# Rotary tables made during the second block's layer-0 closing feed-forward; latent preparation in another order

## What is computed

```python
def second_block(x, mem, positions, ...):
    cos, sin = rope_tables(positions)
    for layer in range(DEPTH_2):
        if layer == N_A_LAYERS:
            shared = shared_mla_kv(x, ..., cos, sin)
        x = x + FFN_HALF * swiglu(rms_norm(x, norm_g[layer, 0]), ...)
        h = rms_norm(x, norm_g[layer, 1])
        if layer < N_A_LAYERS:
            y_mix, q_mem = short_conv_mixer(h, ...)
        else:
            q_nope, q_rope, q_mem = mla_queries(h, ..., cos, sin)
            y_mix = causal_mla_attention(q_nope, q_rope, k_nope, k_rope, v)
        y_mem = memory_attention(q_mem, mem, ...)
        x = x + jnp.concatenate([y_mix, y_mem], axis=-1) @ w_out[layer]
        x = x + FFN_HALF * swiglu(rms_norm(x, norm_g[layer, 2]), ...)

def rope_tables(positions):
    inv_freq = ROPE_THETA ** (-jnp.arange(0, QK_ROPE_DIM, 2) / QK_ROPE_DIM)
    ang = positions[..., None] * inv_freq
    return jnp.cos(ang), jnp.sin(ang)
```

## Time and profile before

| | us |
|---|---|
| median of 3 runs | 3041.64 (3040.64 to 3044.88) |
| the profiled execution, device time | 3040.44 |
| its span, first to last instruction | 3038.2 |
| PE busy | 2986.5 |
| DVE busy | 1828.8 |
| ACT busy | 943.8 |
| POOL busy | 231.7 |
| mean granted clock of PE | 0.996 |

### The profile page before, as it was taken

One profiled execution on the slowest core, in us unless ns is written; L12 is line 12 of the kernel. 1 busy time (PEld: TensorE's weight loads), 2 busy tenths in 40 slices (PEclk: granted clock), 3 DMA queues, 4 the chain that ended last, 5 costly groups with the idle time before them and its releaser, 6 DMA issues.

```text
span 3038.2 us, 36195 instructions
## 1 busy us (share of the span) xinstructions
PE 2986.5 (98%) x13373; PEld 2418.5 (80%) x13373; DVE 1828.8 (60%) x2405; ACT 943.8 (31%) x1279; POOL 231.7 (8%) x107
## 2 busy tenths in 40 slices
PE   8999999999999999999999999999999998999999
PEld 7787788788888887888787888887888875688887
DVE  8896565567766546554587655446554467665532
ACT  4643632333222222222223222222222235322222
POOL 0043240000000000000032000002000022000000
PEclk9999999999999999999999999999999999999999
DMA  4222223233322222223332222332223321122232
GB/s 146 97 93 81 68 97 117 67 103 105 97 97 97 97 97 88 96 95 105 113 107 70 90 97 97 104 104 95 92 97 104 104 87 63 35 90 97 97 104 97
DMA packets 79305, 287.55 MB, mean 95 GB/s; under 512 B 8992, under 2 KB 9248, under 8 KB 78816
## 3 DMA queue, kind: packets, MB, share of 16 engines
q1 hardware_dynamic: 77904, 280.06, 27.5%
q0 software_dynamic: 1296, 6.03, 0.6%
HBM read 283.96 MB, written 2.10 MB: 94 GB/s over the span
## 4 chain that ended last, share of the span: by engine, by line
PE 83%; issue 10%; DVE 5%; POOL 2%; ACT 1%; DMA 0%; POOLq 0%; ACTq 0%; DVEq 0%
PE ps L663 26%; PE ps L665 26%; PE ps L664 26%; POOL w_lo L622 2%; PE ps L1052 1%; PE ps L1297 0%; DVE w_lo L1846 0%; PE ps L1260 0%; DMA mem_x<-in_mem 0%; ACT w_hi L1344 0%; PE ps L833 0%; PE ps L727 0%; PE ps L1041 0%; DVE small L1997 0%; PE ps L947 0%
## 5 line engine op out<-in xcount | busy, mean ns | idle before, releaser
L1344 ACT ACTIVATE w_hi<-raw 128x1024 fp32r<-128x1024 f32 x524 | 554.4, 1058 | 1385.7 <-PE ps L665 1383.5
L663 PE MATMUL ps<-h_hi,w_hi 128*128 128x512 f32 (+1 forms) x2379 | 935.1, 393 | 8.7 <-DVE w_lo L1846 3.3
L665 PE MATMUL ps<-h_hi,w_lo 128*128 128x512 f32 (+1 forms) x2379 | 924.3, 389 | 0.0
L664 PE MATMUL ps<-h_lo,w_hi 128*128 128x512 f32 (+1 forms) x2379 | 924.3, 389 | 0.0
L1846 DVE TENSOR_TENSOR w_lo<-raw,w_hi 128x1024 fp32r<-128x1024 f32 x434 | 530.7, 1223 | 473.9 <-ACT w_hi L1344 473.1
L663 PEld LDWEIGHTS ps<-h_hi,w_hi 128*128 128x128 f32 x2379 | 448.4, 188 | 115.7 <-issue 13.5
L665 PEld LDWEIGHTS ps<-h_hi,w_lo 128*128 128x128 f32 x2379 | 447.8, 188 | 93.0
L664 PEld LDWEIGHTS ps<-h_lo,w_hi 128*128 128x128 f32 x2379 | 448.2, 188 | 92.0 <-issue 2.6
L663 PE MATMUL ps<-mid_hi,w_hi 128*128 128x512 f32 x1208 | 470.8, 390 | 2.2 <-DVE mid_lo L1924 2.1
L664 PE MATMUL ps<-mid_lo,w_hi 128*128 128x512 f32 x1208 | 470.0, 389 | 0.0
L665 PE MATMUL ps<-mid_hi,w_lo 128*128 128x512 f32 x1208 | 470.0, 389 | 0.0
(11 more groups left out here) (409 smaller groups left out, 2471.7 us busy)
## 6 DMA issues: line engine op xcount, KB each, us to landing
raw<-in_wstream SPq DMA_DIRECT2D x525, 512.0 KB, 3.3
x<-in_x SPq DMA_DIRECT2D x4, 512.0 KB, 7.1
x_in<-in_x POOLq DMA_DIRECT2D x8, 256.0 KB, 3.2
mem_x<-in_mem POOLq DMA_DIRECT2D x2, 1024.0 KB, 5.1
out<-x SPq DMA_DIRECT2D x8, 256.0 KB, 4.5
tmp<-in_ret_decay POOLq DMA_DIRECT2D x1, 1024.0 KB, 5.0
rope_r<-in_rope_r POOLq DMA_DIRECT2D x1, 512.0 KB, 3.7
mats<-in_mats SPq DMA_DIRECT2D x1, 256.0 KB, 8.4
```

What stands on the lines that cost most here:

```text
L663: nc.tensor.matmul(dst, hi_w, hi_x, start=first, stop=False)
L664: nc.tensor.matmul(dst, hi_w, lo_x, start=False, stop=False)
L665: return nc.tensor.matmul(dst, lo_w, hi_x, start=False, stop=last)
L1344: nc.scalar.activation(w_hi[:, n % HL], raw[:, r], ACT.Copy).then_inc(hi_ready, 1)
```

## The change

1. POOL loads the positions before the run `conv0`, into `krope` (unused until `ckv`), and waits for them. 2. DVE makes the tables during `s0b_in` through `behind`: conversion, product and first table after pair c = 0, second table after pair c = 1. Work tiles are `ckv`; the result `rope2` lies in the padded rows of the convolution, `cpad`. 3. ACT takes the Sin between `s0b_in` and `s0b_out`. 4. The sums of `cq` come one panel and a half earlier, after the fourth panel of `mla_in`. 5. In `uq` the first two memory panels come first, the last two panels `uq` change places, and the rounds are placed anew; the norms of the last three query tiles come after the first two scores.

```diff
-MEM1_PANEL, MEM1_TILE = (2, 3, 7, 8), (10, 11, 17, 18)
-UQ_PANEL, UQ_TILE = (0, 1, 4, 5, 6), (2, 3, 6, 7, 12, 13, 14, 15, 16)
-V_TILE = (0, 1, 4, 5, 8, 9)
+MEM1_PANEL, MEM1_TILE = (0, 1, 7, 8), (2, 3, 17, 18)
+UQ_PANEL, UQ_TILE = (2, 3, 4, 6, 5), (4, 5, 8, 9, 12, 13, 15, 16, 14)
+V_TILE = (0, 1, 6, 7, 10, 11)
...
-                    rope2 = sb(a, "rope2", [P, 2, S])
...
+        rope2, angle, turns = cpad[:, :, 4:], ckv[:, 0], ckv[:, 1]
...
             pool.dma_start(mem_x[:], A["mem"]).then_inc(side_loaded, 16)
             pool.wait_ge(side_loaded, 48)
+            pool.dma_start(krope[:, 0].bitcast(I32), A["positions"].to_broadcast([P, S])).then_inc(side_loaded, 16)
+            pool.wait_ge(side_loaded, 64)
             split_run("conv0")
...
-            pool.wait_ge(side_loaded, 64)
-            pool.dma_start(rope2[:, 0].bitcast(I32), A["positions"].to_broadcast([P, S])).then_inc(side_loaded, 16)
             pool.wait_ge(side_loaded, 80)
             split_run("mla")
...
                 if j == 1:
                     spread_norms("ckv", "krope")
+                if j == 3:
+                    sums("cq")
...
                 if g == 0:
-                    sums("cq")
-                if g == 1:
                     spread_norms("cq")
             round_sums(1)
...
             v_turned_tiles(0)
-            uq_gemm(0)
+            mem1_gemm(0)
+            mem1_gemm(1)
             round_spread(1)
             round_sums(2)
+            uq_gemm(0)
             v_turned_tiles(2)
+            round_spread(2)
+            round_sums(3)
             uq_gemm(1)
-            round_spread(2)
             v_turned_tiles(4)
-            mem1_gemm(0)
-            mem1_gemm(1)
+            round_spread(3)
+            turn(krope[:, 0])
             uq_gemm(2)
-            round_sums(3)
+            uq_gemm(4)
+            round_sums(4)
             uq_gemm(3)
...
-            ffn("s0b")
+            silus("s0b_in", root)
+            act.wait_ge(sin_in, 2)
+            nc.scalar.activation(rope2, rope2, ACT.Sin).then_inc(sin_done, 1)
+            gemm("s0b_out", to_stage("s0b_out"), parts=3)
...
-            ffn("s0b", gain2(1, 0))
...
+            def rotary_tables(c):
+                if c == 0:
+                    dve.wait_ge(side_loaded, 64)
+                    done(v.tensor_copy(angle, krope[:, 0].bitcast(I32)))
+                    done(v.tensor_scalar(angle, angle, vcol("inv_freq", 0), None, ALU.mult))
+                    rotary_table(0, 0.25)
+                if c == 1:
+                    rotary_table(1, 0.0)
+
+            ffn("s0b", gain2(1, 0), behind=rotary_tables)
```

More of the change, by code:

```diff
@@ L1750, in _ @@
                     drain(st.n + g, st.t + 4 * g + m, (q_nope if m % 2 else k_nope)[:, hd])
[L1751 to L1754, removed]
-                    act.wait_ge(sin_in, 1)
-                    nc.scalar.activation(rope2[:, 0:2], rope2[:, 0:2], ACT.Sin).then_inc(sin_done, 1)
             st = ST["uq"]
@@ L1796, in _ @@
             round_squares(3, qm[:, 0], qm[:, 1], mem_k1_whole)
+            round_root(2)
+            aux[0] += 3
+            uq_drain(0)
+            v_copies(2)
+            round_root(3)
+            aux[0] += 4
+            uq_drain(1)
+            v_copies(4)
+            drained_up_to(UQ_TILE[3])
             uq_drain(2)
-            round_root(3)
-            aux[0] += 3
             drained_up_to(UQ_TILE[4])
             round_squares(4, *(q_rope[:, j] for j in range(3)))
-            uq_drain(3)
+            uq_drain(4)
+            drained_up_to(UQ_TILE[5])
+            round_squares(5, *(q_nope[:, hd] for hd in range(3)))
             round_root(4)
             aux[0] += 3
-            drained_up_to(UQ_TILE[5])
-            round_squares(5, *(q_nope[:, hd] for hd in range(3)))
-            uq_drain(4)
+            uq_drain(3)
+            drained_up_to(UQ_TILE[7])
+            round_squares(6, *(q_nope[:, hd] for hd in range(3, 6)))
             round_root(5)
             aux[0] += 4
-            drained_up_to(UQ_TILE[8])
-            round_squares(6, *(q_nope[:, hd] for hd in range(3, 6)))
             mem1_drain(2)
@@ L2570, in _, with rotary_table @@
             x_gemm("wo0", residual(1.0, "wo0", gain2(0, 2)), 3)
-            ffn("s0b", gain2(1, 0))
+            magic = 1.5 * 2.0 ** 23
+            c1 = 6.28125
+            c2 = float(np.float32(np.round((2 * np.pi - c1) * 2.0 ** 20) / 2.0 ** 20))
+            c3 = 2 * np.pi - c1 - c2
+            def rotary_table(k, quarter):
+                part = rope2[:, k]
+                done(v.tensor_scalar(turns, angle, 1.0 / (2 * np.pi), quarter, ALU.mult, ALU.add))
+                done(v.tensor_scalar(turns, turns, magic, magic, ALU.add, ALU.subtract))
+                done(v.scalar_tensor_tensor(out=part, in0=turns, scalar=-c1, in1=angle, op0=ALU.mult, op1=ALU.add))
+                done(v.scalar_tensor_tensor(out=part, in0=turns, scalar=-c2, in1=part, op0=ALU.mult, op1=ALU.add))
+                done(v.scalar_tensor_tensor(out=part, in0=turns, scalar=-c3, in1=part, op0=ALU.mult, op1=ALU.add))
+                done(v.tensor_scalar(part, part, quarter * 2 * np.pi, 3.1415925, ALU.add, ALU.min))
+                v.tensor_scalar(part, part, -3.1415925, None, ALU.max).then_inc(sin_in, 1)
+            def rotary_tables(c):
[7 more added lines that the diff above has]
+            ffn("s0b", gain2(1, 0), behind=rotary_tables)
             def kv_input(c):
@@ L2607, in _ @@
             split(st.n + 5)
+            reciprocals("cq")
             scaled(st.n + 4, st.t + 4, qm[:, 1])
             split(ST["ukv"].n + 1)
+            dve.wait_ge(panel_done, st.n + 5)
             dve.wait_ge(side_loaded, 80)
[L2612 to L2637 removed]
             memory_input(1, mem_x1, spare[:, 0], mem1_hi, mem1_lo, range(0, 4))
@@ L2651, in _ @@
             gk, gq, gr = vcol("g_k_nope_2", 0), vcol("g_q_nope_2", 0), vcol("g_q_rope_2", 0)
+            memory_input(1, mem_x1, spare[:, 0], mem1_hi, mem1_lo, range(4, 8))
             round_reciprocal(1)
-            memory_input(1, mem_x1, spare[:, 0], mem1_hi, mem1_lo, range(4, 8))
             round_norms(gk, *(k_nope[:, hd] for hd in range(3)))
@@ L2662, in _ @@
             round_reciprocal(5)
-            dve.wait_ge(sin_done, 1)
-            turn(krope[:, 0])
+            turn(q_rope[:, 0])
             round_norms(gq, *(q_nope[:, hd] for hd in range(3)))
             round_reciprocal(6)
-            turn(q_rope[:, 0])
-            round_norms(gq, *(q_nope[:, hd] for hd in range(3, 6)))
-            memory_values(mem_v1, 0)
             def pair_max(at_step, side):
@@ L2677, in pair_outs @@
                     attended(a, tile, out_bank(tile))
+            memory_values(mem_v1, 0)
             pair_max(0, 0)
             pair_max(0, 1)
+            round_norms(gq, *(q_nope[:, hd] for hd in range(3, 6)))
             memory_values(mem_v1, 1)
```

52 lines of the change are left out of this document (12 added, 40 removed).

## The result

| | before | after |
|---|---|---|
| median, us (6 runs each) | 3041.97 (3040.39 to 3044.88) | 3054.36 (3052.96 to 3057.48) |
| ratio after to before | | 1.0043 (95% interval 1.0032 to 1.0053) |
| the profiled execution, device time | 3040.44 | 3054.87 |
| its span | 3038.2 | 3052.7 |

Slower by 12.4 us, 0.4%. The forecast was 3051.0 within 3043.5 to 3057.0.

A forecast was written before the change was run, and what follows sets the result against it. PE, busy 2986.5 of 3038.2 us, bounds the kernel, so only its idle time and clock count. Stops 10.0 plus clock 3.4 minus latent preparation 4.0 make 9.4 us more: 3051.0, range 3043.5 to 3057.0.

The forecast's parts named there:

- Positions ahead of `conv0`: Start of `conv0`: POOL's transfer and wait delay its first `w_lo`, which had no slack; PE stops for 3.7 us.
- Tables: In `s0b_in`, DVE's table blocks delay `w_lo` of panels 3 and 5; PE stops for 3.8 and 2.5 us.
- The Sin: Between `s0b_in` and `s0b_out`: table load and Sin fit ACT's 3.92 us of idle time, 1.6 to spare; costs nothing.
- The clock: PE's clock drops after long stops: 1.7 us for each of two near 3.7, none for 2.5; 3.4 in all.
- The sign that the prediction named: In `s0b_in`, PEclk near 0.5 after PE's first wait for DVE's `w_lo`, the 3.8 us one.
- The latent preparation: From `mla_in` to the first scores: less waiting for DVE, new stops for POOL; gain 4.0 us, between 1.3 and 6.1.
- the layout: Latent preparation, all four lists at row durations and full clock: the old order idles 4.4 us more than the new.
- The sum: Whole kernel: stops 10.0 plus clock 3.4 minus latent preparation 4.0 gives 9.4 us more.
- that the preparation gives all back: Rival, latent preparation: DVE's head start removes all 11.7 us of waits and three clock drops; 3038.2 us, chance 0.12.
- that the stops cost their length alone: Rival, both early stages: the clock keeps its upper level, so 6.0 us more, 3047.6 us; chance 0.17.
- that nothing is gained in E: Rival, latent preparation: POOL and ACT bound it, no gain, third stop costs clock too; 15.1 more, 3056.7 us, chance 0.15.
- the tables hidden in `s0b_in`: Rival, `s0b_in`: PE's start of panel 3 is not the limit, tables cost nothing; 1.4 more, 3043.0 us, chance 0.06.

The follow-up runs named there:

- e1: Kernel before plus one load of the positions ahead of `conv0` into `krope`, read by nothing, POOL waiting for its landing; 3048.07 us, ratio 1.0021.
- e3: The change, positions loaded between POOL's runs `conv0` and `conv`, table blocks behind the second `w_lo` of pairs 1 to 3; 3040.60 us, ratio 0.9996.
- e4: e3 with the kernel before's order of latent preparation; 3039.32 us, ratio 0.9995.
- e10: The change with e7's edit on ACT, load and tables left where the change has them; 3047.46 us, ratio 1.0022.
- e8: The changed kernel itself run once more, for a second profile; 3052.34 us, ratio 1.0032.
- e7: e3 with ACT's rounding of the second memory panel and `uq` panel 3 moved ahead of squares and copies; 3032.17 us, ratio 0.9964.
- e5: Kernel before with the new order of latent preparation only, tables still made by DVE in `mla_in`; 3047.53 us, ratio 1.0017.

## Why the prediction was right

- **Positions ahead of `conv0`, 3.7.** Measured 3.71 in the change, in e1 and in the second profile. The estimate of 2.6 us by the Trainium skill (DMA: Bandwidth & Descriptors, Anatomy of one DMA — SWDGE path) would have missed by 1.1; the row of the same transfer in another place was the better source, and even it was 0.2 above the 3.50 that the transfer then took.
- **Tables, 3.8 and 2.5.** Measured 3.58 and 2.37. The slack read from two rows of DVE and PE and the block's length at undisturbed durations were enough. e3 and e4 confirm what was said of DVE's load: the same instructions one `w_lo` further down in the list cost nothing.
- **The Sin, nothing.** C holds in e3 at 360.96 with the Sin in it. The table load of 1.28 that the prediction put beside it never came: in the change ACT's last Silu starts at 1948.79 and takes 0.61, and the Sin starts at 1949.31 with no load between and 2.97 of idle time behind it. So the cover had more to spare than the 1.6 that was counted.
- **The clock, 3.4: right in sum, wrong in kind.** It was charged as a property of a stop: 1.7 for each near 3.7 us, nothing for 2.5. The runs show it as one of the execution. At `conv0` it came in every profile with the stop: B less the 3.71 of the stop and 0.3 of restart is 1.9 and 1.7 in the change's two profiles, 1.7 in e10 and 2.6 in e1. In C there were none, one or two drops in five profiles with the same stops (0, 1, 1, 2, 2), on average more than the one that I charged; the step's "nothing for that of 2.5" failed in e8 and e10. The sign that the prediction named, PEclk near 0.5 behind the first stop in `s0b_in`, was missing in the change's first profile and there in its second. One more place was charged at nothing and was not: D is 1.1 to 1.6 longer wherever B or C had a stop (and in one profile without). There PE's stop of 1.88 us is an old one, but the four us behind it, at 2124 in the change, have a PEclk of 0.61:

```profile
2124.00:2128.00 4.00, 3.70 (x9) 2.52 (x10) 2.08 (x4) 0.77 (x1) 0.00 (x0) 0.61 0.26 95
```

- **The latent preparation, -4.0: the term that was mis-sized.** It gave 2.2 to 3.0. The low end of my own range, 1.3, came from counting stops in both lists, the high end from laying out all four lists; I took the layout, "since it treats both orders alike". The count was right in each of its rows (3.72 and 2.23 for POOL, 4.4 for the small ones, where 3.7, 2.4 and 4.3 were counted), and its total of 10.4 was met to 0.1. The layout's excess was the number to distrust. The mechanism, w_hi late on ACT and w_lo behind it on POOL, was the right one, and e7 shows that it was worth naming: with the split ahead PE idles 3.6 us less, which is more than the whole of E's gain. e3 and e4 show what the step did not separate: the gain comes from the tables' departure (3.3 us of idle time), and the new order by itself took 1.4 back.
- **The sum.** 9.4 forecast; 12.4 and 9.35 by the medians of two comparisons, 14.5 and 11.0 by the profile of the change against the two of before. Of the 5.1 between 9.4 and 14.5, 3.0 stand in A (clock, but for some 0.3), 1.3 D, 1.8 E and 0.5 B, less 1.5 that C did not take. That the forecast came as near as it did has luck in it: C's 1.5 hides most of E's 1.8, the clock drop charged in C was absent in the profile that was shown and another one stood in D, and A's 3.0, which no sum could have held, is about as large as the distance of the first median from the forecast (3.4).
- **The rivals.** That the preparation gives all back is refuted by E; that the stops cost their length alone holds for C in one profile of five and for B in none; that nothing is gained in E fell too, though its 3056.7 is nearer to the first median (2.3) than the forecast's 3051.0 (3.4), and its mechanism is half true: 5.9 of the 10.3 us of waits there end with POOL behind ACT; the tables hidden in `s0b_in` are refuted by 3.58.

What stays open: why the clock falls behind a given stop in one execution and not in the next, and whether the order of the work moves it. Without an answer the worth of the new order as a whole is known in idle time only (1.4 us lost without the split ahead, 2.2 gained with it), and without the split ahead nothing in these runs speaks for it: the medians of e3 and e4 can't be told apart.

## What to carry to other kernels

Work moved to where an engine is idle on average must be put behind the last instruction that the bottleneck waits for in that engine's list, and the same holds for a transfer whose landing its own queue waits for; both parts of this change cost nothing one step further down. When the wait ends with one engine, ask what that engine itself waited for: POOL was idle for 7 us ahead of the `w_lo` for which PE waited, and two rounding instructions moved up on ACT took away 3.6 us of idle time, with medians 6 to 10 us lower. Before a difference of a few us is explained stage by stage, profile both kernels twice: the kernel before differed from itself by 3.5 us of span.

## What the runs showed of the hardware that was not expected

- The granted clock after one and the same stop differs between executions of the same kernel: 1.00 and 0.62 behind 0.63 and 1.82 us of idle time (before), 1.00 and 0.56 behind 3.58 (the change). A drop lengthened the stage by 1.6 us in C. Stops of 1.9 us were followed by one at some places and in some executions.
- Fewer stops can come with a lower clock. In the first 140 us of E PE idled 13.3 us in e4 and 16.7 in before, and yet got through the same 648 matmuls: PEclk was 0.91 against 0.94. The row of e4, then that of before:

```profile
2443.00:2583.00 140.00, 126.69 (x648) 91.24 (x649) 95.33 (x151) 61.31 (x126) 38.52 (x16) 0.91 0.20 68
```

```profile
2444.00:2584.00 140.00, 123.34 (x648) 89.07 (x647) 105.17 (x166) 64.60 (x129) 39.17 (x17) 0.94 0.21 70
```

- Two of the tables' DVE instructions that started just behind one of POOL's subtractions in e5 ended only after it, as before: the first TENSOR_SCALAR of the first table took 2.50 us there (from 2480.29, POOL's from 2479.91 took 2.60), and 0.43 in the change's `s0b_in`, where POOL is idle.
